# Packed context operands, the first blocks of the next phase written during the phase ahead of it, and regrouped statistics and low parts in a two-model fp32 kernel

## What is computed

```python
hl = xl * (1.0 + sc_l) + sh_l                 # 512 main tokens
hc = xc * (1.0 + sc_c) + sh_c                 # 256 context tokens
parts_l = split(hl @ w_in[l])                 # conv, attention, pooling branches
kc, vc = split(hc @ w_in[l][:, K:V]) if last else ...   # layer 1: keys and values alone
out_l = concat([y_conv, y_attn, y_pool]) @ w_out[l]
xl = layernorm(ALPHA * xl + g_l * out_l)      # xc likewise, in layer 0
```

## Time and profile before

| | us |
|---|---|
| median of 3 runs | 3390.14 |
| lowest, highest | 3390.11, 3390.65 |
| span of the profiled execution, first to last instruction | 3386.8 |
| PE busy in it | 3218.7 (95%) |
| DVE busy | 2245.0 (66%) |
| ACT busy | 1325.1 (39%) |
| POOL busy | 264.5 (8%) |
| mean granted clock of TensorE | 0.978 of full speed |

### The profile page before, as it was taken

The page is one execution under the profiler, slowest core; times in us unless marked ns, Lnnn a source line. Parts: engine busy times, 40 slices in busy tenths (PEclk is TensorE's granted clock), DMA queues, the critical chain, the costliest instruction groups (busy, mean ns, idle before and its releaser), DMA issues.

```text
span 3386.8 us, 48015 instructions
## 1 busy us (share of the span) xinstructions
PE 3218.7 (95%) x16612; PEld 2627.8 (78%) x16612; DVE 2245.0 (66%) x3527; ACT 1325.1 (39%) x2023; POOL 264.5 (8%) x490
## 2 busy tenths in 40 slices
PE   5899999999999999999899999999997999999996
PEld 0799998788777777879788777777785877888885
DVE  0677777766777765676555677774676899755446
ACT  0445555333444443236422444443326222444323
POOL 0000011001101100110101000000110000000000
PEclk7899999999999999999999999999998999999998
DMA  9665556555445433654655444432553322221232
GB/s 398 244 226 208 197 203 244 175 217 189 141 151 165 149 118 125 232 193 161 233 189 203 147 158 146 154 111 77 209 211 116 111 87 94 102 83 70 103 121 87
DMA packets 107407, 554.39 MB, mean 164 GB/s; under 512 B 17856, under 2 KB 17904, under 8 KB 64144
## 3 DMA queue, kind: packets, MB, share of 16 engines
q1 hardware_dynamic: 47232, 343.95, 27.9%
q0 software_dynamic: 60048, 208.75, 18.2%
HBM read 530.55 MB, written 22.04 MB: 163 GB/s over the span
## 4 chain that ended last, share of the span: by engine, by line
PE 72%; DVE 9%; DVEq 6%; DMA 5%; issue 5%; ACT 2%; ACTq 1%; POOL 0%; POOLq 0%; SPq 0%
PE acc L1134 21%; PE acc L1136 20%; PE acc L1135 20%; DVEq L2158 4%; DVE w_lo L1548 3%; PE pv L1256 3%; DMA xy<-in_wm 2%; PE S L1230 2%; DMA gates<-in_wm 2%; PE S L1245 1%; DVE gates L1600 1%; ACT h_hi L624 1%; PE pv L1486 1%; DVE xy L2165 1%; PE misc L1267 1%
## 5 line engine op out<-in xcount | busy, mean ns | idle before, releaser
L1134 PE MATMUL acc<-h_hi,w_hi 128*128 128x512 f32 (+1 forms) x4576 | 1674.2, 366 | 28.6 <-DVE w_lo L1548 19.2
L1136 PE MATMUL acc<-h_hi,w_lo 128*128 128x512 f32 (+1 forms) x4576 | 1643.6, 359 | 0.0
L1135 PE MATMUL acc<-h_lo,w_hi 128*128 128x512 f32 (+1 forms) x4576 | 1642.3, 359 | 0.0
L1134 PEld LDWEIGHTS acc<-h_hi,w_hi 128*128 128x128 f32 x4576 | 867.1, 189 | 185.2 <-issue 44.0
L1136 PEld LDWEIGHTS acc<-h_hi,w_lo 128*128 128x128 f32 x4576 | 867.1, 189 | 129.6
L1135 PEld LDWEIGHTS acc<-h_lo,w_hi 128*128 128x128 f32 x4576 | 867.8, 190 | 128.6 <-issue 6.9
L1548 DVE TENSOR_TENSOR w_lo<-raw,w_hi 128x1024 fp32r<-128x1024 f32 x592 | 697.8, 1220 | 217.9 <-ACT w_hi L624 214.4
L624 ACT ACTIVATE w_hi<-raw 128x1024 fp32r<-128x1024 f32 x592 | 592.8, 1053 | 56.0 <-DMA raw<-in_w 32.2
L624 ACT ACTIVATE ev<-acc 128x512 f32<-128x512 f32 (+1 forms) x210 | 110.6, 530 | 886.2 <-PE acc L1136 866.9
L450 POOL DMA_DIRECT2D gates<-in_wm x288 | 152.9, 531 | 1450.5 <-DVE gates L1600 1257.4
L624 ACT ACTIVATE work<-S,small 128x768 f32<-128x768 f32 (+1 forms) x160 | 129.0, 812 | 256.7 <-DVE small L1712 256.7
(11 more groups left out here) (241 smaller groups left out, 2458.7 us busy)
## 6 DMA issues: line engine op xcount, KB each, us to landing
raw<-in_w SPq DMA_DIRECT2D x296, 1024.0 KB, 4.9
gates<-in_wm POOLq DMA_DIRECT2D x288, 512.0 KB, 4.7
xy<-in_wm SPq DMA_DIRECT2D x32, 1024.0 KB, 8.8
x_d<-xy POOLq DMA_DIRECT2D x2, 4096.0 KB, 13.5
qb<-x_d POOLq DMA_DIRECT2D x16, 256.0 KB, 4.2
kb<-x_d POOLq DMA_DIRECT2D x16, 256.0 KB, 4.2
out_y<-xy POOLq DMA_DIRECT2D x4, 1024.0 KB, 4.1
bias_d<-kb POOLq DMA_DIRECT2D x8, 384.0 KB, 20.3
```

Source lines behind the costliest of these rows:

```text
L1134: mm(o, w_hi[:, w], h_hi[:, x], start=n == 0, stop=False)
L1135: mm(o, w_hi[:, w], h_lo[:, x], start=False, stop=False)
L1136: last = mm(o, w_lo[:, w], h_hi[:, x], start=False, stop=n == len(ks) - 1)
```

## The change

1. **Packed context inputs.** A 256-token block k now lies at column 256k, `c.h` in the lower 4096 columns, the inputs of `cout` and of `kv1` in the upper 4096 (`inputs`, `UPPER`). The lower half is thus free while `cout` and `kv1` run.
2. **Early blocks.** Four pairs (blocks 0 to 7) of `aconv`'s inputs are written after tiles 11 to 14 of `cout`; two pairs (blocks 0 to 3) of `kv1`'s in the last tile of `aout`; four pairs of `bconv`'s in steps 5 and 6 of `kv1`. The last tile of `cout` and `aout` takes its blocks 8 to 15 first, and the stored weights of that tile are rolled to match. The first eight blocks of x have a semaphore of their own (`early_x_land`).
3. **Statistics and low parts.** PE sums the statistics of `aout` after the first pair of `kv1`, and DVE and ACT do the rest of them after that. `w_hi` and `w_lo` of `kv1`'s second tile are made half before and half after the end of `aout`. In the first step of `aconv` and `bconv` one `mod_tiles` piece stands ahead of `w_lo` of the third weight tile where three stood.

```diff
@@ shared
+        whole_early = (evt, t2)
+        def early_pairs(c, i, p):
+            n = 4 * i + p - 11
+            return range(n, n + 1) if c == "c" and isinstance(n, int) and 0 <= n < 4 else ()
+        def early_x(k):
+            return tile(xy, k, SEQ)
-        def y_tile(c, t, k):
-            return t[:, bass.ds(k * SEQ + CTX, CTX)] if c == "c" else tile(t, k, SEQ)
+        UPPER = KT * CTX
+        H_FROM = {"c.h": 0, "c.y": UPPER, "kv1": UPPER}
+        def inputs(c, t, k):
+            T = CTX if c in H_FROM else SEQ
+            return t[:, bass.ds(k * T + H_FROM.get(c, 0), T)]
@@ ACT, project_out
                         f(ev[p][:, 0:T], acc[a.odd][:, 0:T], scale=mod(which, 2, i * 4 + p)).then_inc(acc_free, 1)
+                        for n in early_pairs(c, i, p):
+                            act.wait_ge(early_x_land, shown(early_x_land, 8 * KT))
+                            modulate_pair("a.h", early_x, SEQ, *by_set(0), n, to=whole_early)
...
+                        if ends_a:
+                            act.wait_ge(x_land, shown(x_land, 8 * KT + 16))
+                            act.wait_ge(half_done, shown(half_done, j + 1))
+                            hi(j + 2, (0,))
+                            for n in range(2):
+                                modulate_pair("kv1", ctx_tile, CTX, *by_set(3), n, to=whole_early)
@@ ACT, between phases
-                    act.wait_ge(x_land, shown(x_land, 16 * KT))
+                    act.wait_ge(x_land, shown(x_land, 8 * KT))
+                    hi(At(TILE0["aconv"] + 1))
                     act.wait_ge(tile_done, shown(tile_done, TILE0["aconv"]))
                     act.wait_ge(r_done, shown(r_done, 16))
-                    hi(At(TILE0["aconv"] + 1))
-                    modulate("a.h", lambda i: tile(xy, i, SEQ), SEQ, *by_set(0), 0, KT // 2)
                     modulate("a.h", late_x, SEQ, *by_set(0), KT // 2, KT)
...
-                    hi(At(TILE0["kv1"] + 1))
-                    modulate("kv1", ctx_tile, CTX, *by_set(3))
-                    inverse_deviation("a")
-                    def kv1(i, first=False):
+                    hi(At(TILE0["kv1"] + 1), (1,))
+                    for n in range(2, KT // 2):
+                        modulate_pair("kv1", ctx_tile, CTX, *by_set(3), n, to=whole_early)
+                    def kv1(i, first=False, early=False):
                         for p in range(2):
                             j, a = j_at("kv1", i, p), a_at("kv1", i, p)
                             hi_next(j, p, first)
+                            if early:
+                                modulate_pair("b.h", early_x, SEQ, *by_set(2), 2 * (i - 5) + p)
...
                     kv1(0, first=True)
+                    act.wait_ge(dve_phase, shown(dve_phase, after("aout")))
+                    inverse_deviation("a")
@@ PE
-                            first_pair(j_at("kv1", i, 0), a_at("kv1", i, 0), CTX, H_AT["kv1"])
+                            first_pair(j_at("kv1", i, 0), a_at("kv1", i, 0), CTX, H_AT["kv1"], at=UPPER)
+                            deviation_sums("a")
@@ DVE
+                        elif phase in CHUNK0 and first:
+                            mod_tiles(phase, i, ((0,), (1, 2, 3), (4, 5), (6, 7))[p])
                         elif phase in CHUNK0:
                             mod_tiles(phase, i, ((0, 1, 2), (3, 4, 5), (6, 7), ())[p])
...
+                        if phase == "aout" and k == 7:
+                            dve.wait_ge(x_land, shown(x_land, 8 * KT + 16))
+                            lo(j + 2, (0,))
+                            for n in range(2):
+                                modulate_pair("kv1", ctx_tile, CTX, *by_set(3), n, to=whole_early)
                         dve.wait_ge(tile_done, shown(tile_done, j + 1))
                         stt(new, acc[a.odd][:, :], mod(which, 2, 8 + k), x, ALU.mult, ALU.add).then_inc(acc_free, 1)
...
                     kv1(0, first=True)
+                    finish_stats("a")
@@ host
+    wo0[-1] = np.roll(wo0[-1], D // 2, axis=1)
```

More of the change, by code:

```diff
@@ L1541, in phase_done, with lo @@
                 phases_done[0] += 1
-            def lo(j):
-                for h in range(2):
+            def lo(j, halves=(0, 1)):
+                for h in halves:
                     dve.wait_ge(hi_done, shown(hi_done, j.times(2) + (h + 1)))
@@ L1934, in shifted @@
                             mod_tiles(phase, i, (2 * p, 2 * p + 1))
+                        if phase == "aout" and p == 3:
+                            one_plus((3,), (0, 3 * MOD_COLS) if i == 2 else (3 * MOD_COLS, KT))
                         if k == 0:
@@ L1967, in project_out @@
                     dve.sem_inc(ssum_ready, 1)
-                if phase == "aout":
-                    one_plus((3,))
                 phase_done(phase)
```

134 lines of the change are left out of this document (76 added, 58 removed).

## The result

| | before | after |
|---|---|---|
| median of the runs, us | 3390.12 (4 runs) | 3360.65 (4 runs) |
| lowest, highest | 3387.36, 3390.65 | 3358.38, 3362.42 |
| span of the profiled execution | 3386.8 | 3357.9 |
| PE busy in it | 3218.7 | 3208.0 |

The ratio is 0.9914, with a 95% interval of 0.9902 to 0.9926: faster by 29.5 us, where 27.8 was forecast.

The account below looks back on a forecast made before the run. PE was taken to bound the kernel, so time could come only from its waits and half-rate stretches. Gains of 11.2, 5.1 and 11.5 at three boundaries sum to 27.8, and 3390.1 - 27.8 = 3362.3 us, range 3357 to 3373.

Parts of the forecast that it names:

- Packed inputs: All matmuls on 256-token blocks: the packed layout was costed at nothing, matmuls staying at 120 ns.
- Cover in cout: In cout tiles: an early pair takes DVE about 2.4 us, fits its 2.45 us idle, and costs PE 0.
- cout to aconv: End of cout into aconv: 12.1 us gained less 0.9 for the clock, 11.2, between 7 and 13.
- a similar wait for the fourth piece: DVE in aconv's first step: a wait replacing the earlier 3.18 us piece wait, with 0.5 us estimated gain.
- The clock term: PE in aconv behind the new 2.8 us wait for the squares: half of 1.6 us slow clock, 0.9, lost.
- aout to kv1: End of aout into kv1: last h_lo block 1.8 us earlier plus reordered statistics; gain 5.1, between 2 and 8.
- The gains of order: Early kv1: sums and transposes follow the first pair at once, without the 4.22 us wait; new fourth-tile wait of 1.3.
- kv1 to bconv: End of kv1 into bconv: no idle before the first pair, third tile's piece just in time; gain 11.5, between 8 and 12.
- Half covered: Rival, 3374 us, chance 0.17: slower pairs (2), clock at both new waits (3), late bconv piece (4), smaller kv1 win (3).
- Shoved tiles: Rival, 3383 us, chance 0.04: each of eight 5.75 us tiles grows 2.6 by its early pair, 21 us in all.
- slow packed blocks: Rival, 3406 us, chance 0.03: packed layout adds 10 ns to each of 4224 matmuls, 42 us, net +14.
- More than forecast: Rival, 3356 us, chance 0.06: new waits of 2.8 and 1.3 us do not appear, as DVE starts each chain earlier.

Follow-up runs that it names:

- only_packed: The kernel before with the 256-token blocks packed at 256 columns instead of 512, nothing else; 3389.78 us, ratio 1.0002 to before.
- pairs_a_back: The changed kernel with the four early pairs of aconv's inputs moved back to the start of aconv; 3369.99 us, ratio 0.9941 to before.
- unrolled: The changed kernel with every loop over pairs of blocks in modulate written out on ACT and DVE; 3367.17 us, ratio 0.9933 to before.
- pairs_k_back: The changed kernel with the two early pairs of kv1's inputs moved back behind the last aout tile; 3361.46 us, ratio 0.9915 to before.

## Why the prediction was right, and where not

**Packed inputs: cost 0.** Right: shown by `only_packed` alone.

**Cover in cout: cost 0.** Right. DVE's pair took about 2.05 there (565.25 to 567.29) instead of 2.4 (written out, not in a loop), so even the small margin was larger than read. `cout` tiles kept 5.76.

**cout to aconv, 11.2.** Measured 10.8. The squares' sum came 12.4 us earlier against the last `cout` tile (71.5 before, 59.1 after), forecast 12.1. The new wait was 2.5, forecast 2.8. The weak step was the reading of why. "DVE is the engine that ends last here" was a tie before the change: the sum was ready at 643.7, and PE asked for it at that moment, without a wait.

```profile
643.82 0.70 PE L1386 MATMUL pv<-qb,ones 128*128 128x256 f32 x2
```

That tie is what allowed the whole 12.1 to be counted for PE, and `pairs_a_back` gives back nearly the forecast 10.5. But after the change DVE idles 1.30 for `w_hi` behind PE's first tile and 3.40 for a piece, and the number of pairs no longer counts (`unrolled`). Those 3.40 were allowed for with an estimate of 0.5 and called "a similar wait for the fourth piece"; the wait was in the right place, and it was the one worth removing. The clock term was taken at half, 0.9, and the profiled run paid the full 1.6. The prediction found that "no row before has a wait of this length"; the trace of before had one, 2.38 us ahead of `bconv`'s third tile at 1658.56, with a granted clock of 1.00 in the 4 us behind it.

The Trainium skill (TensorE: Matmul & The Clock Gate, section HAM oscillation) describes a matrix engine whose waits between groups of matmuls make each group start at the lower clock; the waits that it describes are longer than this one. The trace of the changed kernel agrees (granted clock 0.67 in the 4 us behind the wait), three others at this same wait do not (1.00); more is in the last section.

**aout to kv1, 5.1.** Measured 6.4, in the range, but with the split misjudged, so the closeness is partly luck. The last block came 4.6 earlier behind the take of the 15th tile (33.07 before, 28.48 after), where 1.8 was forecast; and the terms listed for it add up to 1531.3, not 1530.4, so to 0.9. The two early pairs gave nothing of this (`pairs_k_back`), since DVE had no idle time in that tile. What the sum left out is that the change writes these pairs out: 1.59 a pair where "2.04 us" was taken from the loop of the earlier trace rows. Eight pairs at 0.45 and the half low part written ahead (1.2) make 4.8, an estimate. Of this, the loop of six pairs was measured: 2.4 on DVE and 1.1 on PE's second tile. The gains of order were forecast at 3.3 net (5.1 - 1.8): PE's wait of 4.22 is gone and a new one of 2.06 stands at the fourth tile, at the place named, where 1.3 was forecast. Given back, they measured 2.2 in B4 and 4.3 by the medians. Some 2 to 3 of the 6.4 had no experiment of their own.

**kv1 to bconv, 11.5.** C3 gives exactly 11.5 (44.52 - 33.02): no idle ahead of the first pair, the piece landing just in time. What the sum missed is one tile further: with three pieces in the second tile, the last of them came 4.99 late, and the fourth tile waited 1.47. At C5 the gain is 10.4. Before the change no row showed this, but the reload of a slot, 3.18 in the earlier trace rows, had the same cause, and the forecast used it in `aconv` only.

**Rivals.** Half covered (3374) is excluded: of its four give-backs only the clock's happened, and in the profiled run at one of the two new waits. Shoved tiles (3383) and slow packed blocks (3406; its own terms give 3404.5) are excluded by 5.76 and by `only_packed`. More than forecast (3356) is not what happened, as both new waits are there.

**The sum.** 10.8, 6.4 and 10.4 make 27.6, forecast 27.8. The medians' 29.5 hold about 2 us that lie in none of the three stretches. The nearness of the sum is better than its parts: the first is 0.4 under, the second 1.3 over and the third 1.1 under.

## What to carry to other kernels

Before writing work ahead into a tile, look for the idle time of each engine in that very tile: four pairs in `cout` tiles with 2.45 us of idle gained 9.6, two pairs in a full `aout` tile gained nothing. Where small loads go through two slots, spread them two to a tile: a third one waits for its slot's reload, and in `aconv` that was the last link of a chain that PE waited for. When an edit removes a link, look at once for the next one (here a load, then a table load ahead of a weight split); three small edits of that kind gave a quarter as much again as the change itself.
